# Streaming the high and low token parts as one 512-column matmul in a split-precision expert layer

## The reference

```python
q = (ht @ w_q).reshape(n_tok, PEER_HEADS, 2, PEER_HALF)      # 1024 -> 2048 queries
s = jnp.einsum('thpd,hpkd->thpk', q, sub_keys)               # scores against 128 sub-keys
s_top, i_top = lax.top_k(s, PEER_TOPK)                       # 16 of 128, two halves
...                                                          # 16 of the 256 pairs
gate = jax.nn.softmax(best, axis=-1)
act = jax.nn.gelu(jnp.einsum('thkd,td->thk', u_tab[eb], xb)) * gb
return jnp.einsum('thk,thkd->td', act, v_tab[eb])
```

## Time and profile before

| | us | share of the span |
|---|---|---|
| median of 3 runs | 2264.95 | |
| the profiled execution, its own time | 2268.4 | |
| its span | 2266.6 | |
| TensorE busy | 2178.9 | 96% |
| VectorE busy | 1476.7 | 65% |
| ScalarE busy | 1342.9 | 59% |
| GpSimd busy | 1069.7 | 47% |

### The profile page before, as it was taken

How to read it: one execution, slowest core, us unless ns; L and a number is a source line. 1 busy time by engine, 2 the same in 40 slices (tenths; PEclk the granted TensorE clock), 3 DMA queues, 4 the chain that set the end, 5 groups by cost and what they waited for, 6 DMA issues and landing times.

```text
span 2266.6 us, 46015 instructions
## 1 busy us (share of the span) xinstructions
PE 2178.9 (96%) x14384; PEld 1984.3 (88%) x14384; DVE 1476.7 (65%) x3206; ACT 1342.9 (59%) x2734; POOL 1069.7 (47%) x827
## 2 busy tenths in 40 slices
PE   7989699999999999999899988999999999999998
PEld 6979599999999988888797767999999999888886
DVE  5756319985666577777765452199756665777776
ACT  6754355577777544444475664555687785444444
POOL 6841378987666600000065337799976665000000
PEclk9989899999999999999999999999999999999999
DMA  5510254555444566666544224555554445666664
GB/s 167 167 58 1 66 176 149 168 165 157 139 139 139 171 190 192 194 194 194 177 133 136 65 66 150 166 159 168 167 155 139 139 139 167 194 193 192 191 194 147
DMA packets 93872, 343.66 MB, mean 152 GB/s; under 512 B 10688, under 2 KB 10752, under 8 KB 93152
## 3 DMA queue, kind: packets, MB, share of 16 engines
q1 hardware_dynamic: 92592, 338.21, 48.5%
q0 software_dynamic: 912, 4.07, 0.6%
q10 hardware_dynamic: 288, 0.34, 0.0%
HBM read 341.53 MB, written 1.05 MB: 151 GB/s over the span
## 4 chain that ended last, share of the span: by engine, by line
PE 82%; POOL 7%; issue 5%; DVE 3%; ACT 2%; DMA 1%; POOLq 0%; DVEq 0%; ACTq 0%
PE bank L359 80%; POOL w_lo L1738 7%; PE bank L524 0%; PE bank L379 0%; DMA small<-in_ssd_d 0%; ACT w_hi L1368 0%; ACT arena L1394 0%; DVE arena L874 0%; ACT arena L1368 0%; DVE arena L989 0%; DVE arena L1190 0%; DVE arena L1029 0%; DVE arena L925 0%; DMA ring<-in_norm_final 0%; ACT arena L1528 0%
## 5 line engine op out<-in xcount | busy, mean ns | idle before, releaser
L1738 POOL TENSOR_TENSOR w_lo<-ring,w_hi 128x512 fp32r<-128x512 f32 x744 | 993.5, 1350 | 685.6 <-ACT w_hi L1368 673.9
L1368 ACT ACTIVATE w_hi<-ring 128x512 fp32r<-128x512 f32 x1280 | 804.4, 630 | 544.5 <-PE bank L359 542.7
L359 PE MATMUL bank<-hT_hi,w_hi 128*128 128x256 f32 x2688 | 780.0, 290 | 9.1 <-POOL w_lo L1738 7.0
L359 PE MATMUL bank<-hT_lo,w_hi 128*128 128x256 f32 x2688 | 761.3, 283 | 0.0
L359 PE MATMUL bank<-hT_hi,w_lo 128*128 128x256 f32 x2688 | 761.2, 283 | 0.0
L359 PEld LDWEIGHTS bank<-hT_hi,w_hi 128*128 128x128 f32 x2688 | 516.2, 192 | 20.1 <-POOL w_lo L1738 19.6
L900 DVE TENSOR_TENSOR w_lo<-ring,w_hi 128x512 fp32r<-128x512 f32 x536 | 374.9, 699 | 220.9 <-ACT w_hi L1368 213.9
L359 PEld LDWEIGHTS bank<-hT_lo,w_hi 128*128 128x128 f32 x2688 | 516.5, 192 | 0.0
L359 PEld LDWEIGHTS bank<-hT_hi,w_lo 128*128 128x128 f32 x2688 | 515.8, 192 | 0.0
L359 PE MATMUL bank<-w_hi,p_ag_hi 128*128 128x512 f32 x1024 | 398.4, 389 | 0.0
L359 PE MATMUL bank<-w_lo,p_ag_hi 128*128 128x512 f32 x1024 | 398.4, 389 | 0.0
(11 more groups left out here) (241 smaller groups left out, 2256.8 us busy)
## 6 DMA issues: line engine op xcount, KB each, us to landing
ring<-in_peer_u SPq DMA_DIRECT2D x256, 512.0 KB, 3.5
ring<-in_peer_v SPq DMA_DIRECT2D x256, 512.0 KB, 3.7
ring<-in_peer_wq SPq DMA_DIRECT2D x32, 512.0 KB, 3.5
ring<-in_gdn_qkv SPq DMA_DIRECT2D x24, 512.0 KB, 3.6
ring<-in_ssd_xbc SPq DMA_DIRECT2D x24, 512.0 KB, 3.6
ring<-in_ssd_z SPq DMA_DIRECT2D x16, 512.0 KB, 3.5
ring<-in_ssd_out SPq DMA_DIRECT2D x16, 512.0 KB, 3.6
ring<-in_gdn_z SPq DMA_DIRECT2D x8, 512.0 KB, 3.5
```

The source lines that it names most:

```text
L359: return pe.matmul(o, w, r, start=first, stop=last)
L1368: return act.activation(o, i, ACT.Copy, scale=scale)
L1738: pool.tensor_tensor(w_part[1][:, s, :], ring[:, n % RING, hf * 512:(hf + 1) * 512], w_part[0][:, s, :].bitcast(F32), ALU.subtract).then_i ...
```

## The change

The high and the low tokens now stand in one tensor `hT_both`. A new `columns_wide` does, for each of the 8 blocks, one matmul of the high weights with 512 columns (256 high and 256 low tokens, to the two halves of the bank) and one of the low weights with 256 columns (high tokens, into the second half). The bank then holds two halves that somebody must add. DVE does that with a `tensor_reduce` over pairs: for the query weights into `p_qT` in ACT's place, for U tiles 56 to 127 into a new tile `p_raw`, from which ACT takes the gelu. On DVE the weighing of a hidden tile moves one tile later, on ACT the one-hot rows of the next map move ahead of the gelu. U tiles 0 to 55 stay as they were.

```diff
+            def columns_wide(bank, n, it=0, step=0, fresh=None):
+                for hf in range(2):
+                    s = half(n, hf, it, step)
+                    for kk in range(KD // 2):
+                        k = KD // 2 * hf + kk
+                        await_h(fresh, k)
+                        c = slice(kk * P, (kk + 1) * P)
+                        mm(bank[:, :].rearrange("p (e t) -> p e t", e=2), w_part[0][:, s, c], hT_both[:, :, k, :], k == 0, False)
+                        last = mm(bank[:, T:2 * T], w_part[1][:, s, c], hT[0][:, k, :], False, k == KD - 1)
+                    last.then_inc(half_used, 1)
...
-                    by_channel(("pq", lyr, m), 4 + m % 2, None if m else 2 * lyr + 1)
+                    columns_wide(PS[4 + m % 2], at[("pq", lyr, m)], fresh=None if m else 2 * lyr + 1)
...
-                columns(PS[i % 2][:, 0:T], n, it, 8)
+                if i < EARLY:
+                    columns(PS[i % 2][:, 0:T], n, it, 8)
+                else:
+                    columns_wide(PS[i % 2], n, it, 8)
...
             def route(lyr):                     # VectorE
+                for m in range(HP):
+                    dve.wait_ge(half_used, 2 * (at[("pq", lyr, m)] + 1))
+                    dve.tensor_reduce(p_qT[:, m, :], PS[4 + m % 2][:, :].rearrange("p (e t) -> p t e", e=2), AX.X, ALU.add).then_inc(SEM["p_q"], 1)
...
+                def add_halves(i, it=0):
+                    dve.wait_ge(half_used, it * 8 + 2 * (tables[lyr] + i + 1))
+                    if not isinstance(it, int) or i > EARLY:
+                        dve.wait_ge(SEM["p_gelu"], it * 4 + (P * lyr + i))
+                    b = PS[i % 2]
+                    dve.tensor_reduce(p_raw, b[:, :].rearrange("p (e t) -> p t e", e=2), AX.X, ALU.add).then_inc(SEM["p_halves"], 1)
...
                     for q in range(4):
+                        i, loop = (EARLY + 4 * it + q, 0) if isinstance(it, int) else (EARLY + q, it)
                         if not first or q:
                             weigh_maps(it, q - 1)
                         if not last or q < 3:
                             one_hots(it, q + 1, first)
-                        if isinstance(it, int):
-                            weigh_hidden(EARLY + 4 * it + q)
-                        else:
-                            weigh_hidden(EARLY + q, it)
+                        if not first or q:
+                            weigh_hidden(i - 1, loop)
+                        add_halves(i, loop)
...
                 weigh_maps(T // 16, -1)
+                for i in range(EARLY + T // 4, P):
+                    add_halves(i)
+                    weigh_hidden(i - 1)
+                weigh_hidden(P - 1)
...
                 parts(0)
                 parts(1)
-                for i in range(EARLY + T // 4, P):
-                    dve.wait_ge(SEM["p_gelu"], P * lyr + i + 1)
-                    dve.tensor_tensor(p_map[:, i, :], p_act[:, i % 2, :], p_map[:, i, :], ALU.mult).then_inc(SEM["p_gated"], 1)
...
             def route(lyr):                     # ScalarE
                 for m in range(HP):
-                    split_half(at[("pq", lyr, m)] + 2, 0)
-                    act.wait_ge(half_used, 2 * (at[("pq", lyr, m)] + 1))
-                    copy(p_qT[:, m, :], PS[4 + m % 2][:, 0:T]).then_inc(SEM["p_q"], 1)
-                    split_half(at[("pq", lyr, m)] + 2, 1)
+                    split(at[("pq", lyr, m)] + 2)
...
-                def late(i, it=0):
+                def late(i, it=0, rows_between=None):
 
                     split_half(n0 + i + 2, 0, it, 8)
-                    act.wait_ge(half_used, it * 8 + 2 * (n0 + i + 1))
+                    if rows_between is not None:
+                        weighed_rows(*rows_between)
+                    act.wait_ge(SEM["p_halves"], it * 4 + ((P - EARLY) * lyr + i - EARLY + 1))
...
-                    act.activation(p_act[:, i % 2, :], PS[i % 2][:, 0:T], ACT.Gelu).then_inc(SEM["p_gelu"], 1)
+                    act.activation(p_act[:, i % 2, :], p_raw, ACT.Gelu).then_inc(SEM["p_gelu"], 1)
                     split_half(n0 + i + 2, 1, it, 8)
```

More of the change, by code:

```diff
@@ L145, in hybrid_encoder @@
         x_sb = sb("x_sb", [P, NT, D])
-        hT = [sb("hT_" + s, [P, KD, T], F32R) for s in ("hi", "lo")]
+        hT_both = sb("hT", [P, 2, KD, T], F32R)
+        hT = [hT_both[:, p, :, :] for p in range(2)]
         ring = sb("ring", [P, RING, D])
@@ L283, in hybrid_encoder @@
         row = [flat(p_ag[0][i * SH:(i + 1) * SH, :, :], "s t") for i in range(2)]
+        p_raw = sb("p_raw", [P, T])[:, :]
         pick = sb("pick", [2 * SH, SH], F32R)[:, :]
@@ L307, in hybrid_encoder @@
             "s_cbps s_cb s_bc s_floor s_logdt masked s_zraw s_e s_sum s_m s_yps s_y s_ss s_mean s_root "
-            "p_q p_sps p_s p_ex p_exd p_key p_Tps p_Tsb p_hot p_hotS p_hotB p_dist p_mapps p_mul p_gelu p_gated p_ag_hi p_ag "
+            "p_q p_sps p_s p_ex p_exd p_key p_Tps p_Tsb p_hot p_hotS p_hotB p_dist p_halves p_mapps p_mul p_gelu p_gated p_ag_hi p_ag "
             "finished stored").split()}
@@ L1678, in hidden_and_rows @@
                     for q in range(4):
+                        rows_between = (it, q + 1, first) if not last or q < 3 else None
                         if isinstance(it, int):
-                            late(EARLY + 4 * it + q)
+                            late(EARLY + 4 * it + q, 0, rows_between)
                         else:
-                            late(EARLY + q, it)
-                        if not last or q < 3:
-                            weighed_rows(it, q + 1, first)
+                            late(EARLY + q, it, rows_between)
                 act.wait_ge(SEM["p_Tsb"], lyr + 1)
```

## The result

The change makes the kernel slower: 2380.15 us (median of 4 runs, 2379.66 to 2382.87) against 2265.38 us for the kernel before in the same job (4 runs). The ratio is 1.0504 [1.0487, 1.0520]. The forecast was 2321 us, with a range of 2290 to 2350: the direction came, and the add behind the map is the reason as foretold, but the size is twice what was forecast (+115 instead of +56 us), and the loop that sets the pace is another one. The profiled execution took 2382.87 us around a span of 2381.1 us.

What follows compares the result with a forecast made beforehand. TensorE was taken to bound the kernel now. Late tiles +27.3, tiles without maps -0.9, hand-over +3.1, query weights -1.4 gave +28.1 us a layer, +56.2 for two: 2264.95 + 56.2 = 2321 us, range 2290 to 2350.

Steps and rivals of the forecast that it cites:

- the tiles without maps: U tiles 121 to 127: they follow TensorE, their add, gelu and split chain being shorter; -0.9 us a layer.
- What bounds the kernel, and the sign: Whole kernel: TensorE bounds it now, in-order engines make it wait after the change; slower, 91% for the rest beyond faster or same.
- The chain of a late step: Late U tiles: map weighing, add, gelu, split, w_lo close over two steps; 4.20 us a step against 3.76, +27.3 a layer.
- the old tile's weighing starts at m + 3.34 and ends at m + 3.75: VectorE's late step, m being the start of the maps on TensorE: hidden-tile weighing precedes the add, which starts at m + 3.90.
- the upper bound for the add: VectorE's add, priced at 0.69 us; upper bound 1766 ns, the longest VectorE form on 512 elements, giving 2392 us, held unlikely.
- The hand-over to V: Last U tile to first V tile: `parts` now wait behind the last add and two weighings; +3.1 us a layer.
- rival (d): TensorE's clock falls: none expected in late tiles, perhaps at the start of V, +2 us a layer; no chance of its own.
- Query weights: Query stage: TensorE bound, 16 units gain 0.11 us each, the last add costs 0.3; net -1.4 us a layer.
- The matmuls: TensorE: 512 plus 256 columns take 0.346 us a block against 0.360; 19 us in all had TensorE remained the bound everywhere.
- (c): Rival, VectorE's add: two-element reduces with 256 results might cost over 1 us, 2340 to 2392 us; 8%.
- (b): Rival, late steps: waits overlap better, the step settles 0.3 us shorter at 3.9 us, 2286 us; 7%.
- (e): Rival, balance: late tiles lose only what the rest wins, a step near 3.8 us, about 2265 us; 3%.

Runs made afterwards that it cites:

- Experiment 2: The changed kernel with VectorE adding tile i's halves first in its late step, then weighing map and hidden tile i; 2264.47 us, ratio 0.9993.
- experiment 1: The changed kernel with the gelu's result in a PSUM bank instead of SBUF (tail weighings also before the next add); 2334.51 us, ratio 1.0303.
- experiment 5: The changed kernel with add first, gelu in PSUM, tiles 121 to 127 as before the change and V's first parts made early; 2251.89 us.
- experiments 1 to 3: The changed kernel with the gelu in PSUM (2334.51 us), with VectorE's add first (2264.47 us), and with both edits (2260.14 us).

## Why the prediction was half right

Where the 114.5 us between the two spans lie, beside the forecast for a layer (in us; what is missing, 0.3 less, lies behind the last V matmul):

| stretch | forecast | layer 0 | layer 1 |
|---|---|---|---|
| before the first query matmul (layer 1: from the last V matmul of layer 0) | 0 | -1.5 | -3.7 |
| query weights, to the first top-k instruction | -1.4 | -0.7 | -1.4 |
| from there to the first map weighing | 0 | -0.2 | -0.2 |
| late steps | +27.3 | +56.1 | +53.8 |
| the tiles without maps, to the last U matmul | -0.9 | -0.6 | -0.6 |
| last U matmul to first V matmul | +3.1 | +4.7 | +4.7 |
| slow matmuls at the start of V | 0 | +2.2 | +2.2 |

*What bounds the kernel, and the sign.* Right. TensorE was the bound, the engines in order decide, and the add behind the weighing of a later map makes TensorE wait. Experiment 2 shows it by changing nothing but VectorE's order.

*The chain of a late step.* Right in its links, and in size once a weighing costs 0.41: experiment 1 gives 4.24 us where 4.20 was worked out. The add's 0.69, taken from a row of another operation with the same 512 elements of a bank, came out at 0.69. Two signals were hardly off: the gelu followed the add by 0.12 or 0.04 us (0.05 taken), and the add followed the weighing by 0.2 (0.15 taken). For which engine TensorE waits was off: mostly for `w_lo`, said the forecast; in experiment 1 it waited 6.8 us for the gelu and 5.1 for `w_lo` between 540 and 740 us, and in the changed kernel 16.2 and 4.1.

*The step that failed* is the sentence "the old tile's weighing starts at m + 3.34 and ends at m + 3.75". Its 0.41 was read from the earlier trace rows, where the weighing falls between two blocks of GpSimd's work. The prediction itself moved GpSimd's work to later, and did not ask what would now run beside the weighing. Its own numbers would have said it: it has a subtraction end at m + 6.92, which is m + 2.72 in the step before, and ScalarE makes the next half unit right behind the one before, so GpSimd goes on until about m + 4.0 (an estimate, 2.72 + 1.30), over a weighing that starts at m + 3.34. The weighing measured 1.42. That is 1.0 us more, and it turned the two-step chain of 4.20 into a one-step loop of up to 4.86; the mean step became 4.66. 56.1 + 53.8 = +110 us stand against the forecast's +55 for these steps, which is nearly the whole miss.

The trace of before had the warning. The parts and weighings behind the maps took very different times for one shape. VectorE's timeline before, at the end of the late tiles of layer 0:

```profile
759.65 0.43 DVE L1326 TENSOR_TENSOR p_ag_lo<-arena,p_ag_hi 128x256 fp32r<-128x256 f32 x1
...
760.31 1.55 DVE L1326 TENSOR_TENSOR p_ag_lo<-arena,p_ag_hi 128x256 fp32r<-128x256 f32 x1
```

And GpSimd's:

```profile
758.17 1.29 POOL L1738 TENSOR_TENSOR w_lo<-ring,w_hi 128x512 fp32r<-128x512 f32 x1 [0.38 <-ACT w_hi L1368]
760.29 1.29 POOL L1738 TENSOR_TENSOR w_lo<-ring,w_hi 128x512 fp32r<-128x512 f32 x1 [0.83 <-ACT w_hi L1368]
```

The first subtraction on VectorE starts after GpSimd's has ended (759.46) and takes 0.43; the second meets the next one (760.29 to 761.58), takes 1.55 and ends 0.28 after it. A spread of one shape between 0.4 and 1.5 us is a reason to look at what else runs.

The Trainium skill, "SBUF — State Buffer", section "Who interferes with whom", states that a VectorE instruction with two SBUF inputs contends with a GpSimd instruction that reads SBUF, and that one with at most one SBUF input (outside VectorE's 2-port modes) or a reduce does not. The runs agree in each case: 1.42 against 0.41 us, and 0.69 for every add of the changed kernel. The prediction drew on another page and passed by this one, although already held a multiplication with two SBUF inputs at 1766 ns. All 32 of those ran beside GpSimd and ended 0.55 us after the end of one of its subtractions; VectorE's own subtraction of the same 512 elements from two SBUF inputs (L900) takes 0.69 in the V stage, where GpSimd is idle. So the row that served as the upper bound for the add was the warning for the weighing.

*The hand-over to V.* Right in kind and too small: from the last U matmul to the first of V it is +4.7 us (831.00 to 835.82, before 0.12) against +3.1, and +2.2 for the clock, which was no term of the sum but rival (d)'s +2. The two weighings there are contended as well. VectorE's timeline after:

```profile
831.99 2.94 DVE L1311 TENSOR_TENSOR arena<-work,arena 128x256 f32<-128x256 f32 x2
```

Rival (d)'s other half is right too: at 177.5 of 200 us busy, the granted clock of the late tiles stayed 1.00.

*Query weights.* Right where a pair took what was forecast: layer 1, with 0.347 us a pair, gained the -1.4 us. Layer 0, with 0.353, gained half of it, -0.7. The first top-k instruction of layer 0 starts 2.2 us earlier (334.77, before 336.97), but 1.5 of these were won before the first query matmul, outside this stage.

*The matmuls.* 512 and 256 columns in 0.346 us was forecast; 0.345 to 0.355 was measured. The gain exists: experiment 5 has 13 of 19 us in the expert layers.

*The other rivals.* The add was not dear (c), the step not short (b), and nothing balanced (e). The case that came, a known instruction that becomes dear because its neighbour moved, was in none of them, and the range of 2290 to 2350 held no term for it. (The 2286 us of (b) takes 0.16 us a step where 3.9 - 3.76 is 0.14; that is 2 us and changes nothing.)

## What to carry to other kernels

When a change shifts an instruction in time, take its duration not from where it stood but from what will run beside it: look for the same shape elsewhere in the trace, and treat a spread in its duration as contention until the rows show otherwise. Put the instruction for which another engine waits first in its step and the one nobody waits for last; here that order alone was worth 115 us, against a gain from fewer matmuls of 13. If two inputs in SBUF contend, moving one to PSUM removes the cost without touching the order. And before a difference of a few microseconds is put down to an edit, see in which stage it lies: here stages with the same work differed by up to 6 us between kernels.

## What the hardware showed unexpectedly

- A VectorE multiplication of 256 elements with two SBUF inputs takes 0.41 to 0.43 us alone and up to 1.54 us beside a subtraction on GpSimd. It ends 0.28 us after the GpSimd instruction it met, whenever it started; one of 512 elements ends 0.55 after. In both, what is left after GpSimd's end is the instruction's own time less 0.14 us (0.42 and 0.69). That it is held until that instruction ends is the reading which fits all of these rows; no run tests it by itself. The Trainium skill, "SBUF — State Buffer", section "Summary: rules for kernel authors", says the same: where VectorE has two SBUF inputs and GpSimd reads SBUF, the second one to issue is fully blocked until the first has finished. The rows agree.
- GpSimd's own subtractions pay less: of the 85 in the late tiles of the changed kernel between 540 and 740 us the median takes 1.29 us and one 1.59. That one starts at 555.97, and the weighing that begins 0.03 us later takes only its 0.41: here it looks as if GpSimd's instruction were the one that is held.
- Matmuls of 512 and of 256 columns in turn start about 0.347 or 0.353 us apart per pair on the mean of a query stage, and the same code shows the one in layer 0 and the other in layer 1; in the late tiles both occur side by side. Neither GpSimd's work nor its absence decides it; the cause is open.
- After 4.5 us without matmuls the next ones ran 0.43 us apart for about ten matmuls, and after waits of 3.5 to 3.9 us (experiments 1 to 3) a slower stretch came too; with TensorE idle 11% of the time in waits of at most 0.5 us the granted clock stayed 1.00.
